# Reading the stored coefficients of two neighbouring tiles in one transfer, in the V stage of a decoder trunk

## The reference, cut to what matters

```
s_half, i_half = lax.top_k(s, TOPK_HALF)
...
gates = jax.nn.softmax(top_s, axis=-1)
...
a = jax.nn.gelu(jnp.einsum('chkd,cd->chk', u_tab[idc], xc).astype(jnp.float32), approximate=False)
coef = (gc * a).astype(xc.dtype)
return jnp.einsum('chk,chkd->cd', coef, v_tab[idc])
```

## Time and profile before

| | |
|---|---|
| median of 3 runs | 3598.56 us (3594.27 to 3604.35) |
| the profiled execution: its time, its span | 3607.47 us, 3605.6 us |
| PE busy, DVE busy, ACT busy, POOL busy | 96%, 85%, 44%, 39% |
| mean granted TensorE clock | 0.986 of full speed |
| V stage of the first layer, of the second | about 1268 to 1800 us, about 3051 to 3590 us |

### The profile page before, as it was taken

One profiled execution on the slowest core, in us unless ns is written; L12 is line 12 of the kernel. 1 busy time (PEld: TensorE's weight loads), 2 busy tenths in 40 slices (PEclk: granted clock), 3 DMA queues, 4 the chain that ended last, 5 costly groups with the idle time before them and its releaser, 6 DMA issues.

```text
span 3605.6 us, 60883 instructions
## 1 busy us (share of the span) xinstructions
PE 3477.3 (96%) x19206; PEld 3172.2 (88%) x19206; DVE 3057.3 (85%) x5845; ACT 1584.9 (44%) x2335; POOL 1391.9 (39%) x1140
## 2 busy tenths in 40 slices
PE   6999999999999999999999999999999999999999
PEld 5766777999999989999977677789999999999999
DVE  6899877999888778888868998779988897888888
ACT  3465434444555433333345644344455554333333
POOL 0000003576666644554500000035856664445442
PEclk9999999999999999999999999999999999999999
DMA  5111263467999999999921122624689999999998
GB/s 193 65 53 58 71 250 118 131 198 252 366 374 353 317 335 347 347 338 349 323 77 59 48 70 88 256 100 149 197 286 378 353 352 326 350 347 341 334 346 282
DMA packets 408599, 863.47 MB, mean 239 GB/s; under 512 B 165520, under 2 KB 231056, under 8 KB 407952
## 3 DMA queue, kind: packets, MB, share of 16 engines
q1 hardware_dynamic: 297456, 539.62, 44.3%
q0 software_dynamic: 73728, 268.47, 20.8%
q10 hardware_dynamic: 37152, 52.45, 3.9%
HBM read 774.41 MB, written 85.98 MB: 239 GB/s over the span
## 4 chain that ended last, share of the span: by engine, by line
issue 58%; POOL 24%; PE 15%; DMA 1%; POOLq 1%; DVE 0%; SPq 0%; ACT 0%; ACTq 0%; DVEq 0%
POOL gbuf L539 10%; POOL w_lo L523 7%; POOL spare L553 7%; PE ps L843 4%; PE ps L844 4%; PE ps L845 4%; DMA raw<-stream 1%; PE ps L589 1%; PE ps L590 1%; PE ps L591 1%; POOLq L552 0%; DMA gbuf<-u_rows,ids_u 0%; POOLq L551 0%; DVE w_lo L1791 0%; DMA gelu_scratch<-g_out 0%
## 5 line engine op out<-in xcount | busy, mean ns | idle before, releaser
L907 ACT CAST w_hi<-raw 128x1024 fp32r<-128x1024 f32 x680 | 715.7, 1055 | 898.7 <-DMA raw<-stream 852.5
L589 PE MATMUL ps<-h_hi,w_hi 128*128 128x384 f32 (+1 forms) x2944 | 1066.7, 362 | 14.1 <-DVE w_lo L1716 11.3
L591 PE MATMUL ps<-h_hi,w_lo 128*128 128x384 f32 (+1 forms) x2944 | 1038.6, 353 | 0.0
L590 PE MATMUL ps<-h_lo,w_hi 128*128 128x384 f32 (+1 forms) x2944 | 1037.8, 353 | 0.0
L843 PE MATMUL ps<-cf_hi,w_hi 128*128 128x384 f32 x2048 | 692.8, 338 | 19.8 <-DVE w_lo L1791 12.7
L845 PE MATMUL ps<-cf_hi,w_lo 128*128 128x384 f32 x2048 | 690.3, 337 | 0.0
L844 PE MATMUL ps<-cf_lo,w_hi 128*128 128x384 f32 x2048 | 690.2, 337 | 0.0
L553 POOL TENSOR_TENSOR spare<-spare 128x1 f32<-128x1 f32 x504 | 333.5, 662 | 794.1 <-DVE y_sp L1770 500.1
L589 PEld LDWEIGHTS ps<-h_hi,w_hi 128*128 128x128 f32 x2944 | 555.7, 189 | 72.2 <-DVE w_lo L1716 16.5
L590 PEld LDWEIGHTS ps<-h_lo,w_hi 128*128 128x128 f32 x2944 | 556.3, 189 | 39.0 <-issue 5.7
L591 PEld LDWEIGHTS ps<-h_hi,w_lo 128*128 128x128 f32 x2944 | 555.3, 189 | 37.7
(11 more groups left out here) (254 smaller groups left out, 4661.5 us busy)
## 6 DMA issues: line engine op xcount, KB each, us to landing
raw<-stream SPq DMA_DIRECT2D x682, 512.0 KB
gelu_scratch<-g_out ACTq DMA_DIRECT2D x256, 192.0 KB
cg<-gelu_scratch SPq DMA_DIRECT2D x256, 192.0 KB
c_scratch<-stage SPq DMA_DIRECT2D x64, 512.0 KB
cg<-c_scratch SPq DMA_DIRECT2D x256, 128.0 KB
qT<-ada SPq DMA_DIRECT2D x32, 512.0 KB
cgate<-ada SPq DMA_DIRECT2D x32, 512.0 KB
w_rows<-ada SPq DMA_DIRECT2D x32, 512.0 KB
```

Source lines behind the costliest of these rows:

```text
L589: nc.tensor.matmul(ps[:, b, 0:n], wh, hi[:, c, t0:T], start=c == 0, stop=False)
L590: nc.tensor.matmul(ps[:, b, 0:n], wh, lo[:, c, t0:T], start=False, stop=False)
L591: mm = nc.tensor.matmul(ps[:, b, 0:n], wl, hi[:, c, t0:T], start=False, stop=c == C - 1)
L907: nc.scalar.copy(w_hi[:, s], raw[:, s]).then_inc(hi_done, 1)
```

## The change

The four buffers cg (c and g of one tile together) become two buffers c_two, each with c of two neighbouring tiles, and four buffers g_in with g of one tile. The transfer of c takes tiles j and j+1 (j even) at once: runs of 512 B in DRAM in place of 256 B, 256 KB in place of 128 KB. It is issued in the odd steps k, for tiles k+5 and k+6, behind raw of tile k+4 and ahead of g of tile k+6, when mix(k+2) is done. g is issued in every step as before. `mix` waits for both, and reads c with a stride between the blocks. Bytes, arithmetic and all other work are the same.

```diff
-        cg = at("cg", base + 74 * KB, [P, 4, NS + ND])
+        c_two = at("c_two", base + 74 * KB, [P, 2, STORED, 2, HALF])
+        g_in = at("g_in", base + 78 * KB, [P, 4, ND])
...
-                def load_cg(s, j, k):
+                def load_c_two(s, j, k):
+
                     jj = sp.snap(j)
                     sp.wait_ge(cg_free, k)
-                    sp.dma_start(cg[:, s, 0:NS].rearrange("i (b t) -> i b t", b=STORED),
-                                 c_scr[:, :, bass.ds(jj, 1)].rearrange("b i o t -> i (b o) t")).then_inc(cg_in[s], 16)
-                    sp.dma_start(cg[:, s, NS:], g_scr[jj]).then_inc(cg_in[s], 16)
+                    sp.dma_start(c_two[:, s].rearrange("i b o t -> i b (o t)"),
+                                 c_scr[:, :, bass.ds(jj, 2)].rearrange("b i o t -> i b (o t)")).then_inc(c_two_in[s], 16)
+
+                def load_g(s, j, k):
+                    jj = sp.snap(j)
+                    sp.wait_ge(cg_free, k)
+                    sp.dma_start(g_in[:, s], g_scr[jj]).then_inc(g_got[s], 16)
...
-                        load_cg(u - NKEYS, u - NKEYS, l * (NKEYS + 4) + u - NKEYS + 1)
-
-                for j in (4, 5):
-                    load_cg(j % 4, j, l * (NKEYS + 4) + j + 1)
+                        j = u - NKEYS
+                        if j % 2 == 0:
+                            load_c_two(j // 2, j, l * (NKEYS + 4) + j + 2)
+                        load_g(j, j, l * (NKEYS + 4) + j + 1)
+
+                load_g(0, 4, l * (NKEYS + 4) + 5)
+                load_c_two(0, 4, l * (NKEYS + 4) + 6)
+                load_g(1, 5, l * (NKEYS + 4) + 6)
...
                         if 32 * r + k + 6 < NKEYS if k1 < 32 else True:
-                            load_cg((k + 2) % 4, 32 * r + k + 6, l * (NKEYS + 4) + 32 * r + k + 7)
+                            if k % 2:
+                                load_c_two((k + 5) // 2 % 2, 32 * r + k + 5, l * (NKEYS + 4) + 32 * r + k + 7)
+                            load_g((k + 2) % 4, 32 * r + k + 6, l * (NKEYS + 4) + 32 * r + k + 7)
...
-                    dve.wait_ge(cg_in[k % 4], (l * (NKEYS // 4) + r + k // 4) * 32 + 32)
+                    dve.wait_ge(c_two_in[k // 2 % 2], (l * (NKEYS // 4) + r + k // 4) * 16 + 16)
+                    dve.wait_ge(g_got[k % 4], (l * (NKEYS // 4) + r + k // 4) * 16 + 16)
                     j = dve.snap(4 * r + k)
-                    nc.vector.tensor_tensor(coef[:, k % 2, 0:NS], cg[:, k % 4, 0:NS], cg[:, k % 4, NS:2 * NS], ALU.mult)
+                    nc.vector.tensor_tensor(coef[:, k % 2, 0:NS].rearrange("i (b t) -> i b t", b=STORED), c_two[:, k // 2 % 2, :, k % 2],
+                                            g_in[:, k % 4, 0:NS].rearrange("i (b t) -> i b t", b=STORED), ALU.mult)
```

More of the change, by code:

```diff
@@ L394, in build_trunk @@
         c_st = sem("c_stored")
-        cg_in = [sem(f"cg_in{s}") for s in range(4)]
+        c_two_in = [sem(f"c_two_in{s}") for s in range(2)]
+        g_got = [sem(f"g_got{s}") for s in range(4)]
         cg_free = sem("cg_free")
@@ L1775, in mix @@
                     dve.wait_ge(cf_ready, l * NKEYS + 4 * r + k + 3)
-                    dve.wait_ge(cg_in[k % 4], (l * (NKEYS // 4) + r + k // 4) * 32 + 32)
+                    dve.wait_ge(c_two_in[k // 2 % 2], (l * (NKEYS // 4) + r + k // 4) * 16 + 16)
+                    dve.wait_ge(g_got[k % 4], (l * (NKEYS // 4) + r + k // 4) * 16 + 16)
                     j = dve.snap(4 * r + k)
-                    nc.vector.tensor_tensor(coef[:, k % 2, 0:NS], cg[:, k % 4, 0:NS], cg[:, k % 4, NS:2 * NS], ALU.mult)
+                    nc.vector.tensor_tensor(coef[:, k % 2, 0:NS].rearrange("i (b t) -> i b t", b=STORED), c_two[:, k // 2 % 2, :, k % 2],
+                                            g_in[:, k % 4, 0:NS].rearrange("i (b t) -> i b t", b=STORED), ALU.mult)
                     nc.vector.tensor_tensor(coef[:, k % 2, NS:].rearrange("i (b t) -> i b t", b=2), stage[:, :, bass.ds(j, 1)].rearrange("i b o t -> i (b o) t"),
-                                            cg[:, k % 4, 2 * NS:].rearrange("i (b t) -> i b t", b=2), ALU.mult).then_inc(cg_free, 1)
+                                            g_in[:, k % 4, NS:].rearrange("i (b t) -> i b t", b=2), ALU.mult).then_inc(cg_free, 1)
                 def mixed_low(k, r):
```

## The result

Over 20 runs each, the changed kernel took 3613.07 us at the median and the kernel before 3598.87 us: a ratio of 1.0033, 95% interval 1.0023 to 1.0044, some 12 us slower. One execution of the changed kernel, of 7357.64 us, is slow and not in the ratio. The forecast was 3604, range 3590 to 3626, with 0.26 on slower by over 0.3%. So 3613.07 lies inside the range, but outside the 3597 to 3609 that the prediction kept for the forecast itself: it is nearest to rival D's 3615.

A forecast was written before the change was run, and what follows sets the result against it. PE was taken as the bound, with DMA near its limit but counting only where PE waits. Terms: -2.4 + 8.0 + 1.3 = +6.9 us, rounded down to +6 on the median of 3598.6: 3604 us, range 3590 to 3626.

The forecast's parts named there:

- rival D: Packets get no cheaper: no relief, odd tiles and starts cost 14.6 + 1.3 = +16 us, 3615; chance 0.06.
- The packets' price: V-stage DMA: each piece carries 9 to 10.6 ns overhead; half the pieces save 0.15 us of DMA time a tile.
- Rival B: DMA relief wins: 512 B go as fast as 256 B, 0.35 us less DMA time a tile, 3594; chance 0.16.
- The late transfer: V stages: w_lo of odd tiles waits behind mix for c landing after its own weights; PE stalls, +8.0 us.
- The lag: How long after the odd tile's weights c lands: taken as 2.0 us, 1.6 with fewer packets.
- the credit of -2.4 us: Shorter waits where PE waits for a landing in V stages: some 0.4 us less at each of six, -2.4 us.
- the six places: Where PE waits for a landing: two in each V-stage start, one near 1560 us and one near 3340.
- Rival C: w_lo of every odd tile becomes the bound; at lag 2.6 us it costs 32 us, 3631; chance 0.22.
- the prediction's table: Odd-tile stalls by lag, two layers: 1.3 us, 0 and 5.4; 1.6, 0.8 and 7.2; 2.6, 13.4 and 19.1.
- W_rows as the cause of late tiles: V stages: late odd tiles are mostly those whose weights stand behind a w_rows block, such as tiles 51 and 99.
- The starts: V-stage starts: -0.6 us at tile 1, first layer; tile 5's w_lo 1.9 us later, second layer; sum +1.3 us.
- The rest: Extra semaphore wait in mix, strided read, fewer SP issues, later weigh and gather: all hidden, no cost.

The follow-up runs named there:

- early pair: Changed kernel with c of two tiles still in one transfer, but issued in the even step behind g of tile k+6: 3601.69 us, 1.0006 of before.
- late 256 B pieces: Changed kernel's late order, but c of the two tiles in two transfers with runs of 256 B: 3614.28 us, 1.0039 of before.
- c behind g: Changed kernel with c issued one place later, behind g of tile k+6 and not ahead of it: 3621.99 us, 1.0068 of before.
- the run with the block moved: Changed kernel with each w_rows block of the loops issued at k%8 == 7 in place of 6: 3612.47 us, 1.0050 of before.
- lateness in the starts alone: Pairs of c issued early, behind g in even steps, except tiles 6 and 7 of each layer, issued late as in the changed kernel: 3599.42 us, 1.0002 of before.

## Why the prediction was right, and where it was off

The range held, the direction was right, and the cause is the one that was named. The size was half of what was measured, +6 for +12 us (interval 8 to 16).

**The bound.** PE sets the end, and a transfer counts only where it makes PE wait: right. Halving the packets and 0.145 us of DMA time a tile changed no time that can be told from zero.

**The packets' price** was right as DMA time (0.15 us a tile taken, 0.145 found). The same window gives an estimate of the price of a piece: the gather queue's 0.345 x 3520 = 1214 engine-us over 53 x 128 rows make 179 ns for 4 KB. Less 59 x 128 of these and 52 x 128 of g, the other queue's 2249 leaves some 450 for 27 x 512 pieces, at most 33 ns each, where a 256 B piece was at most 21.6. The overhead stays with the piece, about 10 ns. Rival B's premise, 512 B in the time of 256, is wrong by this. The Trainium skill ("DMA: Bandwidth & Descriptors", "Specifications") gives 512 B as the least size for line rate; the estimate does not agree, since 512 B at the rate of the 4 KB packets would be 22 ns.

**The late transfer** was the right mechanism: w_lo of odd tiles, behind a mix that waits for c. The early pair has the same pieces and no loss; taking w_lo out from behind mix brings 0.9995, and the same move on the kernel before brings nothing. mix waits some 40 times a layer, not 60, 1.8 us each. PE's waits in the middle are at odd tiles, 0.5 us in the first layer and 2.7 in the second, and in the second profile 0 and 7.6; forecast were 0.8 and 7.2. (The few of the kernel before are at odd tiles too, 83 and 99, so this by itself proves little.)

**The lag** was taken as 2.0 us, 1.6 after relief. In the changed kernel's two profiles the 144 starts of mix with an idle time over 0.2 us come 0.9 us after the odd tile's w_hi at the median, 1.5 in the mean, 5.9 at most. w_lo's end behind w_hi was to be 1.6 + 3.5 = 5.1 us and is 4.8 and 5.0. That fewer packets shorten the lag by some 0.4 us agrees with the run of late 256 B pieces (1.9 us for 1.4 and 1.6). One thing was missed: before, w_lo ended 3.8 us behind w_hi at odd tiles in the mean and not the 3.2 of a tile that finds DVE free. One number for the lag also hides its long tail, as in tile 25.

**The step that failed is the credit of -2.4 us** for shorter waits in the six places. No run shows it: early, 512 B pieces are 1.0006 against 0.9995; late, 1.0032 against 1.0039. These intervals do not exclude it either. In the profiles, PE's waits at tiles 0 to 8 and 64 to 72 of both layers sum to 18.9, 11.0, 13.5 and 7.4 us in the four kernels with early pieces of 256 B and to 8.4 in the early pair: one kernel run twice differs by more than the credit. Without it the sum is 8.0 + 1.3 = +9.3 us, inside the measured interval of 8 to 16. Whether the rest, some 3 us, is noise or a price of the odd tiles that was too low stays open.

**Rival D** has the number, 3615, but not the premise: packets did get cheaper and the lag was not 2.0. That 3615 comes so near 3613 is luck.

**Rival C**, the odd tiles as the bound, was not priced too high. Read with w_lo's end less 3.5 us as the lag, the prediction's table and the 1.3 us of the starts give some 7 to 8 us for the changed kernel, 13 for the late 256 B pieces and 22 with c behind g; measured are 12, 14 and 24 by the ratios, with intervals of some 4, 6 and 7 us on either side.

**W_rows as the cause of late tiles** is not borne out, as the run with the block moved shows. **The starts**, +1.3 us: too small for the run that tried them (1.0002, 0.9991 to 1.0014). **The rest** at nothing: right for the second wait and the stride.

What stays open: the timed loss is 12 us, while PE's waits for w_lo in the middle make 3 to 8 us of single profiles and the kernels before have 0.6 to 1.8. In the run with lateness in the starts alone they make 3.2, with no loss of time. The V stages as a whole say a little more. From the first V matmul to the last, both layers together, the profiles have 1087.0 and 1076.5 us before, 1082.1 and 1093.5 for the changed kernel and 1098.5 with c behind g; the rest of their spans is 2518.6 to 2523.3 us in all five. So what sets these profiles apart lies mostly in the V stages, their starts included, and one profile for each kernel is too coarse to split it further.

## What to carry to other kernels

When two transfers are merged in one in-order queue, the half that was issued earlier moves behind everything between them. Ask what is queued on the consumer's engine behind the instruction that reads it: here the reader itself had time, and the work behind it, w_lo, had not. A saving of DMA time on engines that are nearly full is worth only the stalls that it removes; do not credit it before a row shows them shrinking. And a wait moved twice (earlier issue, later reader) can meet itself in the issuing queue.

## What the runs showed of the hardware that was not expected

Packets of 512 B cost at most 33 ns each and those of 256 B at most 21.6 ns beside a stream of 4 KB packets at 179 ns, so by the estimate above about 10 ns of each is not payload. SP's late issue near tile 68, at the turn of its loop, left 7.75 and 8.54 us between two weight loads before and 7.48 and 6.93 in the changed kernel. PE waited at tile 68 in 4 of 8 V stages of the kernels with early pieces of 256 B, and at tile 67 or 68 in 2 of 18 with pieces of 512 B; at tile 65 it waited in 1 of the 8 and 4 of the 18. Of 0.8 to 3.3 us each, these waits did not show in the time.
